# adaLN projections with 512 moving columns per column group over pairs of chunks, whole transposes, and a sum on VectorE

## The reference

```python
for l in range(2):
    shift, scale, gate = split(silu(c) @ ada_w[l] + ada_b[l], 3)            # (1, 6144)
    shift_c, scale_c, gate_c = split(silu(c_ctx) @ ada_w[l] + ada_b[l], 3)
    h  = rmsnorm(x, norm_g[l]) * (1 + scale) + shift
    hc = rmsnorm(ctx, norm_g[l]) * (1 + scale_c) + shift_c
    # h, hc @ w_in[l]: q, k, v, pool, fourier and gate columns; attention,
    # windowed pooling, 2-D DFT; all times silu(gate columns), @ w_out[l]
    x = x + gate * out                                                       # and ctx alike in layer 0
```

## Time and profile before

| | us |
|---|---|
| median of 3 runs | 2496.76 (2486.05 to 2496.91) |
| the profiled execution's own time | 2492.99 |
| its span from first to last instruction | 2491.2 |
| TensorE busy | 2360.8 (95% of the span) |
| VectorE busy | 1287.7 (52%) |
| ScalarE busy | 1044.9 (42%) |
| GpSimd busy | 195.1 (8%) |
| granted TensorE clock, mean | 0.974 |

### The profile page before, as it was taken

The page is one execution under the profiler, slowest core; times in us unless marked ns, Lnnn a source line. Parts: engine busy times, 40 slices in busy tenths (PEclk is TensorE's granted clock), DMA queues, the critical chain, the costliest instruction groups (busy, mean ns, idle before and its releaser), DMA issues.

```text
span 2491.2 us, 32294 instructions
## 1 busy us (share of the span) xinstructions
PE 2360.8 (95%) x12999; PEld 1893.6 (76%) x12999; DVE 1287.7 (52%) x2086; ACT 1044.9 (42%) x1604; POOL 195.1 (8%) x237
## 2 busy tenths in 40 slices
PE   5889999999999989999998988989999999999998
PEld 2567777677777756787886877868888888888887
DVE  2343433132333255436675786557665666566665
ACT  1232332232322153345654564445553555345543
POOL 1000100000001031100012013230000000000001
PEclk8889999999999999999998999999999999999999
DMA  9764333435665576553354554545655565555652
GB/s 367 271 242 161 127 120 120 121 102 169 192 197 169 169 243 207 186 158 110 117 188 148 173 184 133 174 138 185 186 186 187 185 186 187 186 185 186 187 188 90
DMA packets 347172, 436.78 MB, mean 175 GB/s; under 512 B 13992, under 2 KB 269424, under 8 KB 346128
## 3 DMA queue, kind: packets, MB, share of 16 engines
q1 hardware_dynamic: 341376, 413.19, 52.4%
q0 software_dynamic: 3408, 16.38, 1.8%
q10 hardware_dynamic: 2240, 5.15, 0.6%
HBM read 428.37 MB, written 6.29 MB: 174 GB/s over the span
## 4 chain that ended last, share of the span: by engine, by line
PE 87%; DVE 4%; ACT 3%; DMA 2%; issue 2%; POOL 1%; SPq 0%; ACTq 0%; POOLq 0%; DVEq 0%
PE ps L1121 31%; PE ps L1122 15%; PE ps L1116 5%; PE ps L1102 5%; PE ps L1118 5%; PE ps L1117 5%; PE ps L1104 5%; PE ps L1103 5%; PE ps L1084 3%; PE ps L1182 2%; PE ps L1165 1%; ACT SPL L1299 1%; DVE SPL L1525 1%; DMA RAW<-in_w_in_dram 1%; PE ps L1208 1%
## 5 line engine op out<-in xcount | busy, mean ns | idle before, releaser
L1121 PE MATMUL ps<-HS,SPL 128*128 128x512 f32 x3456 | 1236.3, 402 | 17.2 <-POOL HS L1975 16.5
L1525 DVE TENSOR_TENSOR SPL<-RAW,SPL 128x1024 fp32r<-128x1024 f32 x592 | 726.2, 1233 | 663.9 <-ACT SPL L1299 662.2
L1122 PE MATMUL ps<-HS,SPL 128*128 128x256 f32 x3456 | 972.6, 281 | 0.0
L1299 ACT ACTIVATE SPL<-RAW 128x1024 fp32r<-128x1024 f32 x592 | 621.4, 1057 | 551.6 <-PE ps L1122 351.5
L1121 PEld LDWEIGHTS ps<-HS,SPL 128*128 128x128 f32 x3456 | 654.1, 189 | 183.6 <-POOL HS L1975 16.4
L1122 PEld LDWEIGHTS ps<-HS,SPL 128*128 128x128 f32 x3456 | 657.5, 190 | 2.8 <-issue 2.4
L1102 PE MATMUL ps<-SPL,HS 128*128 128x512 f32 x576 | 245.1, 425 | 23.5 <-DVE SPL L1525 5.6
L1104 PE MATMUL ps<-SPL,HS 128*128 128x512 f32 x576 | 230.7, 400 | 0.0
L1103 PE MATMUL ps<-SPL,HS 128*128 128x512 f32 x576 | 230.5, 400 | 0.0
L1116 PE MATMUL ps<-HS,SPL 128*128 128x512 f32 x512 | 210.4, 411 | 0.9 <-DVE HS L1679 0.9
L1118 PE MATMUL ps<-HS,SPL 128*128 128x512 f32 x512 | 199.6, 390 | 0.0
(11 more groups left out here) (250 smaller groups left out, 1632.6 us busy)
## 6 DMA issues: line engine op xcount, KB each, us to landing
RAW<-in_w_in_dram SPq DMA_DIRECT2D x208, 512.0 KB, 4.8
RAW<-in_ada_w_dram SPq DMA_DIRECT2D x192, 512.0 KB, 4.4
RAW<-in_ffn_w_up_dram SPq DMA_DIRECT2D x192, 512.0 KB, 3.6
RAW<-in_w_out_dram SPq DMA_DIRECT2D x96, 512.0 KB, 4.7
RAW<-in_ffn_w_down_dram SPq DMA_DIRECT2D x96, 512.0 KB, 3.4
x_spill<-XT POOLq DMA_DIRECT2D x2, 2048.0 KB, 14.1
XT<-x_spill POOLq DMA_DIRECT2D x1, 4096.0 KB, 15.7
MM<-in_x_dram ACTq DMA_DIRECT2D x2, 1024.0 KB, 11.8
```

The costliest lines, as they stand in the source:

```text
L1121: mm(PS[b][:, :], wr, hh, start=k == 0, stop=False, skip_group_check=True)
L1122: m = mm(PS[b][:, 256:512], wl, hh[:, 0:256], start=False, stop=k == KT - 1, skip_group_check=True)
L1299: act(SPL[:, (n - 1) % NSPL, 0, :], raw_of(i), ACT.Copy).then_inc(s_hi, 1)
L1525: tt(w[:, 1, :], raw_of(s["i"]), w[:, 0, :].bitcast(F32), ALU.subtract).then_inc(s_lo, 1)
```

## The change

A chunk now has two matmuls of 512 moving columns, one for each of its two row tiles. An even chunk takes column groups 0 and 1 of the array, an odd one groups 2 and 3, so that a pair of chunks fills the four groups that one chunk filled before. Bank 6 then holds eight partial rows (two vectors in four quarters) of 512 columns, summed over the quarters only later. `mixed` puts a pair behind every two main chunks, and `pop_side` takes two tasks ahead of an even ada chunk and none ahead of an odd one. ScalarE copies 512 columns out. `ada_turn` is four whole transposes into bank 7, from which VectorE adds the four quarters (a `tensor_reduce` with its own semaphore) before it adds the bias. `SEL` and its load are gone.

```diff
--- before.py
+++ after.py
@@ -178,7 +177,7 @@
         s_hi, s_lo, s_chunk = sem("split_hi"), sem("split_lo"), sem("chunk_multiplied")
         s_sqx, s_turn, s_xt = sem("x_squares"), sem("x_turned"), sem("x_columns")
         s_ms, s_pow, s_diag, s_rs = sem("mean_square"), sem("rms_power"), sem("rstd_diagonal"), sem("rstd_rows")
-        s_adaE, s_adaT, s_ada, s_s2 = sem("ada_out"), sem("ada_turned"), sem("ada_column"), sem("ada_scale")
+        s_adaE, s_adaT, s_adaS, s_ada, s_s2 = sem("ada_out"), sem("ada_turned"), sem("ada_summed"), sem("ada_column"), sem("ada_scale")
         s_h0, s_h1, s_h1b, s_h2 = sem("h_scaled"), sem("h_hi"), sem("h_shifted"), sem("h_lo")
         s_tg, s_tables, s_qa, s_qd, s_v = sem("rope_cos"), sem("rope_tables"), sem("rows_out_act"), sem("rows_out_dve"), sem("v_out")
         s_nsq, s_nred, s_nms, s_npow = sem("head_squares"), sem("head_sums"), sem("head_means"), sem("head_power")
@@ -302,7 +301,10 @@
                 i = at["pos"]
                 run_ahead()
                 c = chunks[i]
-                pop_side(c.group.side)
+                if c.shape:
+                    pop_side(c.group.side)
+                elif c.kc % 2 == 0:
+                    pop_side(2 * c.group.side)
                 assert str(c.ap) == str(queue[i].ap) and c.shape == queue[i].shape
                 ks = {0: [], 2: range(2 * c.kc, 2 * c.kc + 2), 4: range(4 * c.kc, 4 * c.kc + 4)}[c.shape]
                 inputs = {k: need[c.group.stage](k) for k in ks}
@@ -327,8 +329,9 @@
             seq = []
             for c in main:
                 seq.append(c)
-                seq.extend(left[:1])
-                del left[:1]
+                if len(seq) % 4 == 2:
+                    seq.extend(left[:2])
+                    del left[:2]
             return seq
 
         def alt(i):
@@ -1062,7 +1065,7 @@
             new = Fresh()
             mm, turn = nc.tensor.matmul, nc.tensor.transpose
 
-            e.wait_ge(s_const, 48)
+            e.wait_ge(s_const, 32)
             e.wait_ge(s_vec2, 16 * n_vec2)
             turn(PS[3][:, 0:BW[2]], STAGE[2][0:BW[2], :], IDN[0:BW[2], 0:BW[2]]).then_inc(s_colT, 1)
 
@@ -1079,10 +1082,10 @@
                         for sm, v in new((s_c, 1)):
                             e.wait_ge(sm, v)
                         e.wait_ge(s_raw[i % NRAW], 16 * (i // NRAW + 1))
-                        for q in range(4):
-                            k = 2 * kc + q // 2
-                            m = mm(PS[6][32 * q:32 * q + 32, 0:256], CW[:, 2 * k:2 * k + 32], raw_of(i)[:, q * 256:(q + 1) * 256],
-                                   start=kc == 0, stop=kc == 7, skip_group_check=True)
+                        for kk in range(2):
+                            k, q = 2 * kc + kk, 2 * (kc % 2) + kk
+                            m = mm(PS[6][32 * q:32 * q + 32, :], CW[:, 2 * k:2 * k + 32], raw_of(i)[:, kk * 512:(kk + 1) * 512],
+                                   start=kc < 2, stop=kc >= 6, skip_group_check=True)
                         m.then_inc(s_chunk, 1)
                         continue
                     w = SPL[:, (split_no[i] - 1) % NSPL, :, :]
@@ -1145,9 +1148,9 @@
 
                 elif kind == "ada_turn":
                     e.wait_ge(s_adaE, n)
-                    for q in range(4):
-                        m = mm(PS[7][:, 384 + 2 * q:386 + 2 * q], T(s["slot"])[:, q % 2 * 128:(q % 2 + 1) * 128], SEL[:, q // 2 * 2:q // 2 * 2 + 2],
-                               start=True, stop=True)
+                    for b in range(4):
+                        o = slice(b * 128, (b + 1) * 128)
+                        m = turn(PS[7][:, o], T(s["slot"])[:, o], IDN[:, :])
                     m.then_inc(s_adaT, 1)
 
                 elif kind == "n2":
@@ -1281,7 +1284,6 @@
                 if b == 2:
                     e.dma_start(STAGE[b][r0:r0 + n, :], ap).then_inc(s_vec2, 16)
             e.dma_start(ONES[:, :], I["k_ones"]).then_inc(s_const, 16)
-            e.dma_start(SEL[:, :], I["k_sel"]).then_inc(s_const, 16)
             for t, src in enumerate((I["x"][0, 0:128, :], I["x"][0, 128:256, :], I["ctx"][0, 0:128, :], I["ctx"][0, 128:256, :])):
                 e.dma_start(MX[:, t, :], src).then_inc(s_x[t], 16)
             e.wait_ge(s_memset, 2)
@@ -1306,7 +1308,7 @@
                 elif kind == "ada_out":
                     for sm, v in new(*s["last"]):
                         e.wait_ge(sm, v)
-                    act(T(s["slot"])[:, 0:256], PS[6][:, 0:256], ACT.Copy).then_inc(s_adaE, 1)
+                    act(T(s["slot"]), PS[6][:, :], ACT.Copy).then_inc(s_adaE, 1)
 
                 elif kind == "h1":
                     l, k, src = s["l"], s["k"], s["s"]
@@ -1552,9 +1554,11 @@
                     a = ADA[:, l, 4 * g:4 * g + 4, :]
                     c = c_adb + 48 * l + 4 * g
                     e.wait_ge(s_adaT, n)
+                    nc.vector.tensor_reduce(a, PS[7][:, :].rearrange("p (b q r) -> p b r q", b=4, q=4)[:, :, 0:2, :], AX_X, ALU.add).then_inc(s_adaS, 1)
                     for sm, v in new((s_col, 3)):
                         e.wait_ge(sm, v)
-                    tt(a, PS[7][:, 384:392].rearrange("p (q v) -> p q v", v=2), VV[:, c:c + 4].unsqueeze(2).to_broadcast([P, 4, 2]), ALU.add).then_inc(s_ada, 1)
+                    e.wait_ge(s_adaS, n)
+                    tt(a, a, VV[:, c:c + 4].unsqueeze(2).to_broadcast([P, 4, 2]), ALU.add).then_inc(s_ada, 1)
                     if 4 <= g < 8:
                         c = c_norm + 16 * l + 4 * (g - 4)
                         e.wait_ge(s_ada, n)
```

More of the change, by code:

```diff
@@ L78, in two_block_program @@
         SM = sb("SM", [P, 64])
-        SEL = sb("SEL", [P, 4])
         PS = [es.enter_context(nc.psum_tensor(f"ps{b}", [P, 512], F32)) for b in range(8)]
@@ L2026, in shape_constants @@
     k = {"k_idn": np.eye(128, dtype=f), "k_ones": np.ones((128, 128), f), "k_tril": np.tril(np.ones((128, 128), f))}
-    k["k_sel"] = np.tile(np.kron(np.eye(2), np.eye(32, 2)), (2, 1)).astype(f)
     inv = (f(10000.0) ** (-np.arange(0, 64, 2, dtype=f) / f(64))).astype(f)
```

## The result

The changed kernel takes 2512.33 us (median of 5 runs, 2507.65 to 2517.99), the kernel before 2496.76 (2486.05 to 2498.03): a ratio of 1.0074, 95% interval 1.0052 to 1.0095. It is slower by 15.6 us, where the forecast was no change. Its profiled execution took 2514.06 us, 21.1 more than that of before.

A forecast was written before the change was run, and what follows sets the result against it. TensorE was taken to bound the kernel wherever the weight stream doesn't. Terms of -21.0 - 5.6 + 13.8 + 6.0 + 11.3 - 3.1 + 1.7 = +3.1 on 2492.99 gave 2496.1 us, range 2480 to 2514.

The forecast's parts named there:

- Bound by PE: Whole kernel: TensorE work and waits set the time wherever the weight stream doesn't; it is busy 95% of the span.
- Terms 1 and 2: Ada work on TensorE: 60 pairs each save a 0.35 us visit, -21.0 us; 16 shorter turns save 0.35 each, -5.6.
- Term 3: Ends of layer 0's two q groups and layer 1's kv group: n2 waits uncovered for its norm chain, +13.8 us.
- term 5: Side tasks standing together without an ada chunk between: 18 such neighbours in layer 0 wait longer, +11.3 us.
- Term 4: Behind the three new norm waits: TensorE runs at low clock, 2.0 us lost at each, +6.0 us.
- Small ones: Layer 1's attention burst loses waits, -3.1 us; wider ScalarE copies and later loads at the start, +1.7; VectorE's reduce hidden.
- A: Norm chains at group ends: the saving stands and they cost nothing, nor does the clock; 2476 us, chance 0.14.
- B: Layer 1's ada pairs starve for weights: four of 12 wait 2 us and lose 2 to clock, +16, 2512 us; chance 0.15.
- C: Ada pairs on TensorE: the two halves don't run side by side, +0.86 us for 68 pairs, +58, 2554 us; chance 0.05.
- D: The new turns: whole transposes let TensorE's clock fall, 16 x 2.0 = +32 us, 2528 us; chance 0.02.

The follow-up runs named there:

- The turn alone: Kernel before with only the turn changed, two whole transposes and two VectorE sums in place of the SEL matmuls: 2482.52 us, ratio 0.9947.
- One idle row: Changed kernel with one empty side task behind the second norm row of each q and kv group: 2491.61 us, ratio 0.9974.
- the norm rows apart: Changed kernel with empty side tasks behind the second and third norm rows of each q and kv group: 2478.37 us, ratio 0.9934.
- the form alone: Kernel before with 512-column ada matmuls and the new turn, but single ada chunks in the old order: 2527.81 us, ratio 1.0119.
- runs of four: Old-form, one-task pair kernel with four ada chunks behind four w_out chunks in layer 0 instead of two behind two: 2511.22 us, ratio 1.0055.

## Why the prediction was wrong

The forecast was no change, 2496.1 us, and the kernel is slower by 15.6. The mechanism of the price was foreseen, and how often it is paid was not.

**Bound by PE: right.** The difference stands in PE's work, waits and clock; between 163 and 674 us the DMA share fell to 0.37 from 0.43.

**Terms 1 and 2, fewer visits and the turn: right.** 60 x 0.375 and 16 x 0.30 measured for 0.35 each. The turn alone showed a shorter one that the term hadn't asked about, at 0.22.

**Term 3, three norm chains: its sizes were right, its count was not.** This is the step that failed: "three norm chains lose their cover". The three it named waited 5.65, 5.65 and 6.24 us for a predicted 5.5, 5.5 and 5.9; less the 4.1 us that stood there before, that is +13.4 for a forecast 13.8. But the same rule, two tasks at each pair, reaches the later norm rows as well. I followed the row at a group's end and took the others as side neighbours of term 5 at 0.78 each, because in the trace of before they waited only for a PSUM bank. The traces show 2.42 us before the fourth `n2` of each q group in layer 0, 4.92 before the last one ahead of layer 1's kv group, and 3.20 where 0.58 stood. These sum to 12.4 us over what before had there. One idle row cured the three named waits and the one of 4.92, two cured those of 2.42 as well; only the 3.20 stayed, at 2.84, and what makes it is open. With the norm rows apart the kernel was 34.9 us shorter up to chunk 359, where terms 3 and 4 together had +19.8. The missing 15.1 would have made the forecast 2511.2.

**Term 4, the clock: right in kind, somewhat low, not in place.** The clock that wasn't granted in PE's busy time from 163 to 1200 us rose by 8.8 us, from 11.5 to 20.3, for a forecast 6.0. The 3.20, 4.11 and 4.92 us waits of layer 1 had one low stretch of 17 us over them where before had one of 7, a few short waits had stretches of their own, and one at the attention burst went.

**Term 5, side rows: about right.** Waits of over 0.3 us on lines other than `n2` rose by 6.2 us from 163 to 1200 us, from 26.6 to 32.9. Without the burst's gain of 1.0 and the two bank waits like that of the earlier trace rows that went, it is +9.3, and the short waits of `n2` rows that this term counts come on top, for a forecast 11.3.

**Small ones.** The burst of layer 1 gained 4.6 us at chunk 359 (predicted 3.1); one wait of 1.68 took the place of 2.68, where I wrote none. At the end of chunk 71 the changed kernel was 1.3 us ahead, for a predicted loss of 1.7; the profiled executions differ by up to 5 there.

The books, for the two profiled executions: -22.5 - 4.8 for terms 1 and 2, +38.5 for all waits of over 0.3 us from 163 to 1200 us (32.6 before, 71.0 after) and +8.8 for the clock make +20.0, and the ends of chunk 359 lie 20.3 apart. The two executions lie 21.1 apart, the medians 15.6.

**The rivals.** A (the norm chains cost nothing) is refuted by the waits, but its price came out for a kernel without most of them: 2476 forecast, 2478.4 measured with the norm rows apart. B's figure of 2512 was met for another reason: PE's wait for the ada loads, 7.7 us, is 6.9 in after, and the large waits between 890 and 1056 us are `n2`'s. C (the halves don't run side by side) is out (its 68 pairs should have been 64, which makes its price 55 and its time 2551): four records of a pair are side by side in 0.64 us,
```profile
606.38 0.64 PE L1087 MATMUL ps<-RAW,CW 128*32 128x512 f32 x4
```
and a pair takes 1.00 us where a lone chunk of the form alone takes 0.98. The second chunk has a wait for its own load between its records and the first chunk's, and its records stand beside them all the same. The Trainium skill, TensorE: Matmul & The Clock Gate, Part 3, says that matmuls keep strict program order in start and end. The trace doesn't contradict that: the first records of the four matmuls of this pair start in turn within 0.02 us, and their second records, 0.45 us later, end in turn within 0.02 us. What is out is the reading that I hung on it, that both records of one matmul must be over before the next column group begins; it gave a pair five steps of 0.43. D (transposes let the clock fall) is out: from 313 to 674 us the granted clock is 1.00 with 103 transposes of 128x128 in it, 20 of them the new turns' (the window from 163 to 674 of before held 136, not hundreds). From 163 to 1200 us low clock stands behind waits alone.

**The margin.** 2512.3 lay inside the range of 2480 to 2514 and over 2509, where I had put 0.20. That the range held is luck: B had widened it, and the error of the count was not foreseen. Nor was the sign: the forecast said no change, and the interval of the ratio is clear of 1.

## What to carry to other kernels

When steps that were popped one by one come to be popped in twos, write out every chain of dependent side tasks in the new order, to the last row of each, and compare its length on the other engines with what PE has between its parts; the one at the group's end isn't the only one. Halving how often a resource is visited and halving how often side work is served are two changes: keep the first, and give the second its own rate. Here pairs of ada chunks with one side task each, and two transposes for a turn, take 2468.25 us, 1.2% under before, while the wider matmuls that the pairs were made for bring about 0.05 us a pair, no more than their longer turn costs. And look where grouped work lies against the groups of the main stream: runs of four behind groups of four put every split behind the end of a group.

## What was new about the hardware

- Column groups that run side by side cost next to nothing to each other: two of four busy took 0.98 us, four of four 1.00, for the same 512 columns.
- The two records of a matmul on 32-bit floats don't stand one behind the other when four column groups are used: the eight weight loads of a pair start within 0.05 us, then four matmul records together, one of each group, and 0.45 us later the other four.
- Halving the number of ada matmuls gave almost nothing in itself: a pair stands 0.05 us closer to the next (12.09 against 12.14). Against the same order with twice as many matmuls of half the columns, the wider form's medians were 2.3 and 3.2 us higher, within the spread of the runs and of the size of its longer turn (16 x 0.22).
- Two equal waits of 5.65 us had unequal prices behind them: the next 4.0 us were granted 0.60 of the clock in one place, the next 6.0 us 0.52 in the other, so the same wait lost another 1.6 us (4.0 x 0.40) and 2.9 (6.0 x 0.48).
- Two short waits in a row can do it too, and not each time: 0.83 and 1.18 us at 693 to 695 were followed by a granted clock of 0.57 over 4 us, 0.97 and 0.95 at the same step of before by 1.00.
